# Quarter-array matmuls for filter generation and RG-LRU gates, odd magnitudes on VectorE

## The chip, the cores and the metric

The kernel runs on one core of one Trainium2 chip. The metric is the device time of one execution in microseconds (us), the median of the runs. TensorE multiplies, VectorE (DVE), ScalarE (ACT) and GpSimd (POOL) work on vectors, and SyncE (SP), ACT and POOL issue transfers (DMAs).

## The reference, cut to what matters

One encoder block over 2048 tokens of 1024 channels, all in float32. Half of the mixer is an RG-LRU (a gated linear recurrence, forward and backward), half a Hyena operator (long convolutions with filters that a small network makes). Then comes a mixture of experts, which the change does not touch.

```
# filters: k = [hf, 0, reversed hb], then divided by its own absolute sum
z = sin(ff2 * (z @ fw2 + fb2))                       # 64 features per position
h = (z @ fw3).reshape(seq, 2, 2, 512) * exp(-t * deltas)
k = concat([h[:, 0], 0, h[1:, 1][::-1]])
k = k / (sum(abs(k)) + EPS)
# gates: 8 heads of 64 channels, block-diagonal weights, for each direction
r = sigmoid(einsum("bshi,hij->bshj", xh, wr) + br)
i = sigmoid(einsum("bshi,hij->bshj", xh, wi) + bi)
a = exp(-8 * r * softplus(-lam));  b = sqrt(1 - a*a) * (i * xc)
h = scan(a, b)                                       # forward, and backward with its own weights
```

## The kernel before

Every engine runs its own instruction list in program order, and semaphores are the only links between the lists. The program is a sequence of phases. The change touches two of them, and what it queues on POOL reaches into a third.

**Filters (`norm_and_filters`).** The filter of 4096 positions is worked through in 32 tiles `j` of 128 positions by 2 orders by 512 channels. For each tile TensorE makes the values (`generate`, L229, into one of two PSUM buffers `pk`), DVE multiplies them by the decay table (L374, into one of four buffers `kt`, or `kt0` for tile 0), ACT takes the magnitude (L303, into `ka[j % 2]`), POOL adds it to a running sum (L200), TensorE multiplies the tile by a transform matrix (`transform`, L243), and ACT copies that out (L309) for a store by SP. `zzd` holds the features of both filter halves as a block-diagonal operand padded with zeros, so that one matmul contracts over 128 rows. Every second tile ACT and DVE also split one slice of the normalised input into a high and a low part (`h_hi`, L319; `h_lo`, L355). TensorE issues `generate(j)`, then `transform(j - 2)`; `generate(j)` waits for L374 of tile `j - 2`. After tile 31 TensorE multiplies the sum by ones, DVE adds the skip term to `kt0` (L379, L382), and the last transform follows.

**Projection and RG-LRU (`project_and_lru`).** TensorE projects 20 tiles of 128 channels (L521, 96 matmuls each, in 4 chunks of 512 tokens with one PSUM bank each). Four of them are lru inputs `("x", c)`, four are lru gates `("g", c)`. For every `c`, four gate products of 4 chunks (L534: weights r and i, forward and backward) go through the same 4 banks. Each matmul takes two 64x64 heads as one 128x128 block-diagonal weight `WG`. ACT evacuates them with a sigmoid (L591) into `T` and `I`, DVE multiplies by `xc` (`weigh`, L725), ACT makes decay terms (L634 to L637), DVE scans (L735). The list for one `c` on DVE: `weigh` twice, `lru_input`, forward scan, `low`, `lru_input`, backward scan, `add_directions` (L739), `lru_conv(c + 1)`, `low`, `gate_result` (L744), which signals `y_ready`. ACT begins the sigmoids of `c + 1` when `y_ready` comes. The gates of `c = 0` are interleaved with other work; those of `c` = 1, 2, 3 stand together behind the projection of `("g", c - 1)`. A group of gates also needs the convolved input of its own `c` (`xc_ready`).

**Long convolution (`conv`).** It starts while `c = 3` is being finished. DVE runs the last backward scan after its first block of products (`scan_last`), the sum of directions after its fourth (`add_last`). POOL makes the real part `yr` of each block (L1050, L1054), which TensorE's `inverse` (L957) waits for. This phase's code follows `project_and_lru`'s on every engine.

Of the kernel before, what the change touches and what calls it, by code (L numbers as in the profile page):

```python
# [109 lines left out]
def norm_and_filters(nc, dram, h_hi, h_lo, X, invn, ident):  # L110
# [7 lines left out]
    with ExitStack() as ctx:  # L118
# [5 lines left out]
        zzd = sb("zzd", [P, 2, SEQ])  # L124
# [3 lines left out]
        w3, fa, ones = sb("w3", [P, 2, CH]), sb("fa", [P, P]), sb("ones", [P, P])  # L128
        dec = sb("dec", [P, 4, CH])
# [5 lines left out]
        skip = dec[0:1, 0:2, :]  # L135
# [9 lines left out]
        kgen, k_ready, abs_ready, summed, fa_done, kst_ready = (sem(n, 0) for n in ("kgen", "k_ready", "abs_ready", "summed", "fa_done", "kst_ready"))  # L145
# [10 lines left out]
        def _(sp):  # L156
# [14 lines left out]
            sp.dma_start(fa[:, :], dram["fa_filter"]).then_inc(f_in, 16)  # L171
# [5 lines left out]
            for j in range(N2):  # L177
                if j >= 4:
                    sp.wait_ge(k_ready, j - 3)
                sp.dma_start(dec[:, j % 4, :], dram["decay"][:, j, :]).then_inc(dec_in[j % 4], 16)  # L180
                if j >= 5:
                    store(j - 5)
            sp.wait_ge(k_ready, N2 - 2)
            sp.dma_start(skip, dram["hy_skip"]).then_inc(skip_in, 16)
# [6 lines left out]
        def _(pool):  # L191
# [5 lines left out]
            for j in range(N2):  # L197
                pool.wait_ge(abs_ready, j + 1)
# [4 lines left out]
        def _(pe):  # L203
# [19 lines left out]
            view = zzd.rearrange("p h (q l) -> p l h q", l=N2)  # L223

            def generate(j):
                if j >= 2:
                    pe.wait_ge(k_ready, j - 1)
                for o in range(2):
                    last = pe.matmul(pk[j % 2][:, o, :], view[:, j], w3[:, o, :], start=True, stop=True)  # L229
                last.then_inc(kgen, 1)  # L230

            def transform(i):
# [3 lines left out]
                else:  # L236
                    pe.wait_ge(k0_ready, 1)
# [4 lines left out]
                for o in range(2):  # L242
                    last = pe.matmul(pa[i % 2][:, o, :], fa[:, :], tile(j)[:, o, :], start=True, stop=True)  # L243
# [20 lines left out]
        def _(act):  # L264
# [30 lines left out]
            act.activation(zzd[0:R, 0, :], arg[0:R, :], ACT.Sin).then_inc(mlp_sin, 1)  # L295
            act.activation(zzd[R:P, 1, 1:SEQ][:, ::-1], arg[R:P, 1:SEQ], ACT.Sin).then_inc(mlp_sin, 1)
            turned(FIRST, NT)

            def magnitude(j):
# [3 lines left out]
                act.activation(ka[j % 2], tile(j), ACT.Abs).then_inc(abs_ready, 1)  # L303
# [20 lines left out]
        def _(dve):  # L324
# [32 lines left out]
            dve.memset(zzd[R:P, 0, :], 0.0)  # L357
            dve.memset(zzd[0:R, 1, :], 0.0)
            dve.memset(zzd[R:P, 1, 0:1], 0.0)
# [8 lines left out]
            for j in range(N2):  # L368
                dve.wait_ge(dec_in[j % 4], 16 * (j // 4) + 16)
                dve.wait_ge(kgen, j + 1)  # L370
                if j >= 5:
                    dve.wait_ge(fa_done, j - 4)
                    dve.wait_ge(abs_ready, j - 3)
                dve.tensor_tensor(tile(j), pk[j % 2][:, :, :], dec[:, j % 4, :].unsqueeze(1).broadcast_to([P, 2, CH]), ALU.mult).then_inc(k_ready, 1)  # L374
# [3 lines left out]
            dve.wait_ge(skip_in, 16)  # L378
            dve.scalar_tensor_tensor(out=skip, in0=pk[0][0:1, :, :], scalar=EPS, in1=skip, op0=ALU.add, op1=ALU.mult).then_inc(norm_ready, 1)  # L379
            dve.wait_ge(norm_ready, 1)  # L380
            dve.wait_ge(abs_ready, 1)
            dve.tensor_tensor(kt0[0:1, :, :], kt0[0:1, :, :], skip, ALU.add).then_inc(k0_ready, 1)  # L382
# [13 lines left out]
def project_and_lru(nc, dram, h_hi, h_lo, invn, ident, ps, marks):  # L396


    with ExitStack() as ctx:
# [14 lines left out]
        PT = sb("PT", [P, N_Q + 2, CT])  # L414
# [26 lines left out]
        steps = sem("p_steps")  # L441

# [6 lines left out]
        marks.update(xraw=xraw, WG=WG, fs=fs, mm_done=mm_done, evac=evac, tr_evac=tr_evac, xc_ready=xc_ready, sa_out=sa_out,  # L449
# [58 lines left out]

        @block.tensor
        def _(pe):  # L510
# [16 lines left out]
            def gate(c, g):  # L527
# [43 lines left out]
            for j in range(13, len(TILES)):  # L571
                project(j)
                if TILES[j] in GATED:
                    for g in range(4):
                        gate(GATED[TILES[j]], g)

        @block.scalar
        def _(act):
            col = lambda q, c: PT[:, q, c:c + 1]

# [1450 lines left out]
```

## Time and profile before

| | us |
|---|---|
| median of 3 runs (2303.22 to 2306.31) | 2304.76 |
| the profiled execution | 2303.28 |
| its span in the profile | 2301.5 |
| busy in the span: TensorE / DVE / ACT / POOL | 2068.6 / 1221.4 / 1115.4 / 345.9 |
| filter tiles, first to last `generate` | about 69 to 174 |
| projection and RG-LRU | about 198 to 775 |

The span runs from the first to the last instruction. The granted TensorE clock has a mean of 0.955 of full speed. A matmul of float32 operands stands as two passes in the trace. Starts in the rows are us from the span's start.

### The profile page before, as it was taken

Reading aid. Unit: us, or ns where it says so; the run is one execution under the profiler, and the core shown is the slowest. Engines: PE = TensorE matmul, PEld = TensorE weight load, DVE = VectorE, ACT = ScalarE, POOL = GpSimd, SP = SyncE. Lnnn points to the kernel's source line nnn. Section 1 sums busy time; section 2 is a strip of 40 time slices with the busy share of each in tenths; the row PEclk is TensorE's granted clock in tenths of the full one; section 3 lists DMA queues with packets and bytes.
Section 4 is the critical chain, followed back from the end, with each engine's and each line's share of the span. In section 5 each row is a group of like instructions: output and inputs, shape, how many; then the busy total and the mean of one; then the engine's idle time right before and its main releaser. Section 6 shows DMA issues by size and latency. Waiting matters only on the chain. (4 is left out here: it accounts for less than half of the span.)

```text
span 2301.5 us, 30650 instructions
## 1 busy us (share of the span) xinstructions
PE 2068.6 (90%) x9069; PEld 1500.0 (65%) x9070; DVE 1221.4 (53%) x1111; ACT 1115.4 (48%) x1315; POOL 345.9 (15%) x309
## 2 busy tenths in 40 slices
PE   3996999999999997878999669999999999999990
PEld 1654787786666421226878558888788788888870
DVE  7552322223666654663444475466868655664643
ACT  6762222225555532342333145466867765665643
POOL 0560000000000230220000011212111121221120
PEclk9997999999999999998999769999999999999995
DMA  5461213213111699757542356787999987886858
GB/s 190 157 226 62 64 55 92 73 37 94 39 38 38 244 341 348 273 192 249 178 165 96 128 193 196 249 275 252 374 310 375 374 293 222 297 284 207 291 145 313
DMA packets 239629, 462.08 MB, mean 201 GB/s; under 512 B 24897, under 2 KB 87461, under 8 KB 235174
## 3 DMA queue, kind: packets, MB, share of 16 engines
q1 hardware_dynamic: 201798, 375.17, 45.6%
q0 software_dynamic: 14400, 52.44, 9.5%
q10 hardware_dynamic: 23360, 33.56, 4.5%
q8 instruction: 42, 0.69, 0.1%
q14 instruction: 29, 0.23, 0.0%
HBM read 346.79 MB, written 114.29 MB: 200 GB/s over the span
## 5 line engine op out<-in xcount | busy, mean ns | idle before, releaser
L1762 PE MATMUL p<-wh_hi,x_hi 128*128 128x512 f32 x768 | 309.0, 402 | 1.7 <-DVE x_lo L1876 0.6
L1762 PE MATMUL p<-wh_hi,x_lo 128*128 128x512 f32 x768 | 304.4, 396 | 0.0
L1762 PE MATMUL p<-wh_lo,x_hi 128*128 128x512 f32 x768 | 304.2, 396 | 0.0
L1888 DVE TENSOR_TENSOR wh_lo<-w_raw,wh_hi 128x2048 fp32r<-128x2048 f32 x128 | 284.8, 2286 | 27.6 <-ACT wh_hi L1849 27.6
L521 PE MATMUL ps<-h_hi,wp_hi 128*128 128x512 f32 x640 | 257.7, 403 | 15.3 <-DVE wp_lo L698 15.3
L521 PE MATMUL ps<-h_lo,wp_hi 128*128 128x512 f32 x640 | 254.6, 398 | 0.0
L521 PE MATMUL ps<-h_hi,wp_lo 128*128 128x512 f32 x640 | 254.3, 397 | 0.0
L1849 ACT ACTIVATE wh_hi<-w_raw 128x2048 fp32r<-128x2048 f32 x128 | 234.8, 1924 | 0.4 <-DMA w_raw<-in_exp_w_dram 0.4
L1050 POOL TENSOR_TENSOR arena<-arena 128x512 f32<-128x512 f32 x32 | 56.9, 1778 | 762.4 <-DVE arena L1066 762.4
L1762 PEld LDWEIGHTS p<-wh_hi,x_hi 128*128 128x128 f32 x768 | 144.9, 189 | 35.6 <-issue 1.7
L1762 PEld LDWEIGHTS p<-wh_hi,x_lo 128*128 128x128 f32 x768 | 145.0, 189 | 35.2
L1762 PEld LDWEIGHTS p<-wh_lo,x_hi 128*128 128x128 f32 x768 | 145.0, 189 | 32.8
L1762 PE MATMUL pyy<-wy_hi,a_hi 128*128 x392 | 159.9, 408 | 5.9 <-ACT yb L1833 4.7
L1762 PE MATMUL pyy<-wy_hi,a_lo 128*128 x392 | 155.8, 398 | 0.0
L1762 PE MATMUL pyy<-wy_lo,a_hi 128*128 x392 | 155.6, 397 | 0.0
L521 PEld LDWEIGHTS ps<-h_hi,wp_hi 128*128 128x128 f32 x640 | 121.4, 190 | 46.5 <-DVE wp_lo L698 16.9
L1888 DVE TENSOR_TENSOR wy_lo<-w_raw,wy_hi 128x2048 fp32r<-128x2048 f32 x64 | 144.2, 2286 | 8.8 <-ACT wy_hi L1849 8.8
L1903 DVE TENSOR_TENSOR a<-p,s 128x512 f32<-128x512 f32 x48 | 33.2, 691 | 214.6 <-ACT s L1862 214.6
L521 PEld LDWEIGHTS ps<-h_lo,wp_hi 128*128 128x128 f32 x640 | 121.3, 190 | 29.5 <-issue 1.0
L521 PEld LDWEIGHTS ps<-h_hi,wp_lo 128*128 128x128 f32 x640 | 121.2, 189 | 29.5
L589 ACT ACTIVATE hraw<-ps 128x512 f32<-128x512 f32 x48 | 28.7, 599 | 221.0 <-PE ps L521 221.0
L1849 ACT ACTIVATE wy_hi<-w_raw 128x2048 fp32r<-128x2048 f32 x64 | 120.8, 1923 | 25.0 <-DMA w_raw<-in_exp_w_dram 21.5
(300 smaller groups left out, 3537.0 us busy)
## 6 DMA issues: line engine op xcount, KB each, us to landing
w_raw<-in_exp_w_dram SPq DMA_DIRECT2D x512, 256.0 KB, 5.9
w_raw<-in_exp_w_dram SPq DMA_DIRECT2D x128, 512.0 KB, 10.7
scratch_KA<-work SPq DMA_DIRECT2D x32, 512.0 KB, 3.0
scratch_SI<-arena SPq DMA_DIRECT2D x32, 512.0 KB, 3.4
kin<-scratch_KA SPq DMA_DIRECT2D x21, 512.0 KB, 6.1
arena<-scratch_SA SPq DMA_DIRECT2D x21, 512.0 KB, 5.1
wp_raw<-in_w_in_dram SPq DMA_DIRECT2D x20, 512.0 KB, 3.8
h_raw<-in_x_dram ACTq DMA_DIRECT2D x4, 2048.0 KB, 20.2
```

The lines of the kernel that those rows point to most:

```text
L521: last = pe.matmul(out, w[:, s, k, :], h, start=(k == 0 and i == 0), stop=(k == KC - 1 and i == 2))
L589: ins = act.activation(out[:, 512 * n:512 * (n + 1)], pj[n], func)
L1050: dif = pool.tensor_tensor(yr[:, n % 2, :], by_r[:, n % 2, 0, :], by_i[:, n % 2, 1, :], ALU.subtract)
L1762: mm = pe.matmul(acc[:, :], x[:, k, :], w, start=(k == 0 and i == 0), stop=(k == n - 1 and i == 2))
L1849: act.activation(place, raw[:, j:j + 2, :], ACT.Copy).then_inc(rounded, 1)
L1888: dve.tensor_tensor(lo, raw[:, j:j + 2, :], hi.bitcast(F32), ALU.subtract).then_inc(lowered, 1)
L1903: dve.tensor_tensor(a[:, :], p3[:, :], s1[:, :], ALU.mult).then_inc(a_ready, 1)
```

## The change

The filter values and the gates of `c` = 1, 2, 3 come out of 64x64 quarters of the array, four to a group: two row halves by two column halves. Quarters on the diagonal keep a head (or a filter half) on its partitions; the others put it on the opposite half of the partitions. So half of the results lies swapped.

- Filters: `zz` without padding, four quarter matmuls per tile; order 1 has its partition halves swapped, so the decay table and the transform matrix get a second, swapped copy (512 KB per tile instead of 256 KB). Magnitudes of odd tiles move from ACT to DVE as max(-k, k). The skip term is added in two pieces.
- Gates: for each kind and chunk, four quarters into two banks, forward straight, backward swapped. The backward direction then uses `PT_swapped` and `xc_swapped`, and the result of the backward scan is swapped back. All exchanges are pairs of SBUF to SBUF transfers issued by POOL. `xc_swapped` lies in `xraw`, so its next filling waits for `weighed`.
- On DVE `add_directions(c)` moves behind `lru_conv(c + 1)` and `low`, and waits for `exchanged`.

```
-                    last = pe.matmul(pk[j % 2][:, o, :], view[:, j], w3[:, o, :], start=True, stop=True)
+                    for h in range(2):
+                        rows, out = slice(R * h, R * h + R), slice(R * (h ^ o), R * (h ^ o) + R)
+                        last = pe.matmul(pk[j % 2][out, o, :], view[rows, j], w3[rows, o, :], start=True, stop=True)
...
-            magnitude(1)
...
-                magnitude(j)
+                if j % 2 == 0:
+                    magnitude(j)
...
+                if j % 2:
+                    dve.wait_ge(k_ready, j + 1)
+                    if j >= 3:
+                        dve.wait_ge(summed, j + 1)
+                    dve.scalar_tensor_tensor(out=ka[1], in0=tile(j), scalar=-1.0, in1=tile(j), op0=ALU.mult, op1=ALU.max).then_inc(abs_odd, 1)
...
+            def exchange(out, a, done):
+                for h in range(2):
+                    pool.dma_start(out[halves[h]], a[halves[1 - h]]).then_inc(done, 16)
+
+            pool.wait_ge(lam_ready, 1)
+            exchange(PT_swapped, PT, pt_swapped)
+            for c in range(1, CT):
+                pool.wait_ge(xc_ready, c + 1)
+                exchange(xc_swapped, xc, xc_exchanged)
+                pool.wait_ge(scanned, 2 * c + 2)
+                exchange(I[1], T[1], exchanged)
...
+            def gate_quarters(c):
+                pe.wait_ge(xc_ready, c + 1)
+                pe.wait_ge(wg_in, 16 * 8 * (c + 1))
+                for kind in range(2):
+                    for n in range(NCHUNK):
+                        u = kind * NCHUNK + n
+                        b = 2 * (u % 2)
+                        pe.wait_ge(evac, after(gate_place[c] + u // 2 - 1, b + 1))
+                        for d in range(2):
+                            for h in range(2):
+                                rows, out = halves[h], halves[h ^ d]
+                                last = pe.matmul(pj[b + d][out, :], WG[rows, 2 * d + kind, R * h:R * h + R], xc[rows, n * 512:(n + 1) * 512],
+                                                 start=True, stop=True)
+                            last.then_inc(mm_done, 1)
...
-                dve.wait_ge(evac, after(gate_place[c] + 2 * d + 1))
-                step(dve.tensor_tensor(I[d], I[d], xc, ALU.mult))
+                dve.wait_ge(evac, after(gate_place[c] + (3 if c else 2 * d + 1)))
+                if c and d:
+                    dve.wait_ge(xc_exchanged, 32 * c)
+                    dve.tensor_tensor(I[d], I[d], xc_swapped, ALU.mult).then_inc(weighed, 1)
+                    dve.wait_ge(weighed, c)
...
                 lru_scan(1)
-                add_directions(c)
+                if c == 0:
+                    add_directions(c)
                 lru_conv(c + 1)
                 low(TILES.index(("g", c)) + 1)
+                if c:
+                    add_directions(c)
                 gate_result(c)
```

The built order of instructions shows three places.

On DVE in the filter tiles, before (two tiles; L374 is the decay product, L355 the low part):

```order
L374 TENSOR_TENSOR work<-fk,dec 128x1024 [waits fa_done,abs_ready,kgen,dec_in2]
L355 TENSOR_TENSOR h_lo<-h_raw,h_hi 128x1024 [waits h_high]
L374 TENSOR_TENSOR work<-fk,dec 128x1024 [waits fa_done,abs_ready,kgen,dec_in3]
L374 TENSOR_TENSOR work<-fk,dec 128x1024 [waits fa_done,abs_ready,kgen,dec_in0]
L355 TENSOR_TENSOR h_lo<-h_raw,h_hi 128x1024 [waits h_high]
```

and with the change (L378, L358; L383 is the magnitude of an odd tile):

```order
L378 TENSOR_TENSOR work<-fk,dec 128x1024 [waits fa_done,abs_even,kgen,dec_in2]
L358 TENSOR_TENSOR h_lo<-h_raw,h_hi 128x1024 [waits h_high]
L378 TENSOR_TENSOR work<-fk,dec 128x1024 [waits abs_odd,fa_done,kgen,dec_in3]
L383 SCALAR_TENSOR_TENSOR ka<-work 128x1024 [waits summed,k_ready]
L378 TENSOR_TENSOR work<-fk,dec 128x1024 [waits fa_done,abs_even,kgen,dec_in0]
```

The magnitude stands behind the product of its tile and waits for POOL's sum of the tile two before.

On DVE behind the backward scan of `c = 1`, before (L739 adds the directions, L704 and L706 are the convolution, L744 gates the result):

```order
L735 SCALAR_TENSOR_TENSOR hraw<-tst,hc 128x2048 [waits p_steps]
L739 TENSOR_TENSOR hraw<-hraw 128x2048 [waits scanned]
L704 TENSOR_SCALAR hc<-xraw,PT 128x2048 [waits evac,p_steps]
L706 SCALAR_TENSOR_TENSOR hc<-xraw,PT,hc 128x2048 [waits p_steps] x3
L698 TENSOR_TENSOR wp_lo<-wp_raw,wp_hi 128x1024 [waits w_high]
L744 TENSOR_TENSOR tst<-hraw,spread 128x64x32 [waits evac]
```

and with the change:

```order
L797 SCALAR_TENSOR_TENSOR hraw<-tst,hc 128x2048 [waits p_steps]
L761 TENSOR_SCALAR hc<-xraw,PT 128x2048 [waits evac]
L763 SCALAR_TENSOR_TENSOR hc<-xraw,PT,hc 128x2048 [waits p_steps] x3
L755 TENSOR_TENSOR wp_lo<-wp_raw,wp_hi 128x1024 [waits w_high]
L803 TENSOR_TENSOR hraw<-hraw,hc 128x2048 [waits exchanged,scanned]
L808 TENSOR_TENSOR tst<-hraw,spread 128x64x32 [waits evac,p_steps]
```

The sum moved from before the convolution to behind `low`, with a wait for the exchange.

On POOL, what stands between the sums of the filter phase and the first `yr` of the long convolution, with the change; before, the two memsets were all there was:

```order
L521 MEMSET prow 128x128
L522 MEMSET WG 128x512
L526 DMA PT_swapped<-PT 64x108 [waits lam_ready]
L526 DMA PT_swapped<-PT 64x108
L526 DMA xraw<-hc 64x2048 [waits xc_ready]
L526 DMA xraw<-hc 64x2048
L526 DMA hc<-hraw 64x2048 [waits scanned]
L526 DMA hc<-hraw 64x2048
```

The last four rows come three times, for `c` = 1, 2, 3. So POOL's first `yr` now stands behind a wait for the last backward scan and two transfers.

## Rows read from the trace of the kernel before

**Rows 1.** The page: busy time, share of the span, instructions of each engine.

```profile
PE 2068.6 (90%) x9069; PEld 1500.0 (65%) x9070; DVE 1221.4 (53%) x1111; ACT 1115.4 (48%) x1315; POOL 345.9 (15%) x309
```

**Rows 2.** Windows: length, busy PE, PEld, DVE, ACT, POOL, clock, DMA share, GB/s.

```profile
120.00:150.00 30.00, 30.00 (x72) 17.12 (x71) 14.98 (x13) 21.53 (x23) 20.36 (x10) 1.00 0.72 236
```

**Rows 3.** Timeline of two filter tiles: start, us, engine, line, operation, [idle before, releaser].

```profile
112.42 1.22 DVE L374 TENSOR_TENSOR work<-fk,dec 128x1024 f32<-128x1024 f32 x1 [1.04 <-issue]
...
113.88 1.88 PE L229 MATMUL fk<-w,zzd 128*128 128x512 f32 x4
...
114.81 2.35 POOL L200 TENSOR_TENSOR acc<-acc,ka 128x1024 f32<-128x1024 f32 x1 [1.07 <-ACT ka L303]
...
115.60 1.88 PE L243 MATMUL fp<-work,fa 128*128 128x512 f32 x4
...
115.86 1.22 DVE L374 TENSOR_TENSOR work<-fk,dec 128x1024 f32<-128x1024 f32 x1 [2.21 <-PE fk L229]
...
117.00 1.25 DVE L355 TENSOR_TENSOR h_lo<-h_raw,h_hi 128x1024 fp32r<-128x1024 f32 x1
117.11 1.06 ACT L303 ACTIVATE work<-work 128x1024 f32<-128x1024 f32 x1 [1.46 <-DVE work L374]
```

**Rows 4.** Timeline of the early filter tiles, DVE and POOL side by side.

```profile
81.11 2.37 POOL L200 TENSOR_TENSOR acc<-acc,ka 128x1024 f32<-128x1024 f32 x1
...
82.68 1.88 DVE L355 TENSOR_TENSOR h_lo<-h_raw,h_hi 128x1024 fp32r<-128x1024 f32 x1
...
83.93 2.85 POOL L200 TENSOR_TENSOR acc<-acc,work 128x1024 f32<-128x1024 f32 x1 [0.45 <-ACT work L303]
```

**Rows 5.** Timeline of TensorE in the long convolution, half-array matmuls.

```profile
1012.99 1.89 PE L933 MATMUL ps<-kin,fwd_b 128*64 128x512 f32 x8
1014.81 1.99 PE L957 MATMUL ps<-arena,inv_b 64*128 64x512 f32 x8
1016.72 1.94 PE L944 MATMUL ps<-arena,fwd_b 128*64 128x512 f32 x8
```

**Rows 6.** Timeline of ACT around the gates of `c = 1`.

```profile
610.65 0.60 ACT L589 ACTIVATE spread<-ps 128x512 f32<-128x512 f32 x1 [5.00 <-PE ps L521]
...
615.03 2.42 ACT L591 ACTIVATE hraw<-ps,PT 128x512 f32<-128x512 f32 x4 [2.19 <-DVE tst L744]
...
620.36 0.69 ACT L591 ACTIVATE hraw<-ps,PT 128x512 f32<-128x512 f32 x1 [0.17 <-PE ps L534]
...
627.08 1.28 ACT L634 ACT_TABLE_LOAD   x1
```

**Rows 7.** Timeline from there to the next gates, ACT and DVE.

```profile
633.60 1.91 ACT L637 ACTIVATE hraw<-hraw 128x2048 f32<-128x2048 f32 x1
...
643.16 0.60 ACT L589 ACTIVATE xraw<-ps 128x512 f32<-128x512 f32 x1 [4.05 <-PE ps L521]
...
654.64 4.43 DVE L735 TENSOR_TENSOR_SCAN hraw<-tst,hc 128x2048 f32<-128x2048 f32 x1
...
671.79 3.72 DVE L744 TENSOR_TENSOR tst<-hraw,spread 128x2048 f32<-128x2048 f32 x1 [0.72 <-ACT spread L589]
```

**Rows 8.** A window of 2 us at the start of the long convolution, TensorE alone.

```profile
782.00:784.00 2.00, 1.30 (x4) 0.50 1.11 455
```

**Rows 9.** Timeline there: POOL, DVE, TensorE.

```profile
780.16 4.95 POOL L1054 COPY arena<-arena 1x512 f32<-1x512 f32 x1
780.30 4.41 DVE L735 TENSOR_TENSOR_SCAN hraw<-tst,hc 128x2048 f32<-128x2048 f32 x1
...
786.31 2.94 PE L957 MATMUL ps<-arena,inv_b 64*128 64x512 f32 x8
```

**Rows 10.** A group of POOL's by form: busy us, mean ns of one.

```profile
L1728 POOL DMA_INDIRECT scratch_X<-yb,curspot x50 | 80.3, 1606 | 41.4 <-POOL curspot L1725 39.7 <-PE px L1770 1.7
```

**Rows 11.** Transfers: out<-in, queue, count, KB each, median us to landing.

```profile
scratch_YT<-tst SPq DMA_DIRECT2D x3, 1024.0 KB, 5.1
...
scratch_X<-yb,curspot POOLq DMA_INDIRECT x50, 9.2
```

More of the change, by code:

```diff
@@ L134, in norm_and_filters @@
         ka, acc, kt0 = [kst[:, 3], split(ka1)], split(acc_flat), split(gain)
-        skip = dec[0:1, 0:2, :]
+        skip = [dec[R * o:R * o + 1, 0, o, :] for o in range(2)]
         pair = lambda name: ctx.enter_context(nc.psum_tensor(name, [P, 2, CH], F32))
@@ L183, in _ @@
             sp.wait_ge(k_ready, N2 - 2)
-            sp.dma_start(skip, dram["hy_skip"]).then_inc(skip_in, 16)
+            for o in range(2):
+                sp.dma_start(skip[o], dram["hy_skip"][:, o, :]).then_inc(skip_in, 16)
             for i in range(N2 - 5, N2):
@@ L242, in transform @@
                 for o in range(2):
-                    last = pe.matmul(pa[i % 2][:, o, :], fa[:, :], tile(j)[:, o, :], start=True, stop=True)
+                    last = pe.matmul(pa[i % 2][:, o, :], fa[:, o, :], tile(j)[:, o, :], start=True, stop=True)
                 last.then_inc(fa_done, 1)
@@ L377, in _ @@
             dve.wait_ge(norm_mm, 1)
[L378 to L382, printed above, removed]
+            dve.wait_ge(skip_in, 32)
+            for o in range(2):
+                dve.scalar_tensor_tensor(out=skip[o], in0=pk[0][R * o:R * o + 1, o, :], scalar=EPS, in1=skip[o], op0=ALU.add, op1=ALU.mult).then_inc(norm_ready, 1)
+            dve.wait_ge(norm_ready, 2)
+            dve.wait_ge(abs_even, 1)
+            for o in range(2):
+                first = kt0[R * o:R * o + 1, o, :]
+                dve.tensor_tensor(first, first, skip[o], ALU.add).then_inc(k0_ready, 1)
             for i in range(NT - 2, NT):
@@ L441, in project_and_lru @@
         steps = sem("p_steps")
+        pt_swapped, xc_exchanged, weighed, exchanged = (sem(n, 0) for n in ("pt_swapped", "xc_exchanged", "weighed", "exchanged"))
+        halves = [slice(R * h, R * h + R) for h in range(2)]
         w_v = dram["w_in"].rearrange("o (k p) n -> p (o k) n", p=P)
@@ L573, in _ @@
                 if TILES[j] in GATED:
-                    for g in range(4):
-                        gate(GATED[TILES[j]], g)
+                    gate_quarters(GATED[TILES[j]])
         @block.scalar
@@ L642, in sigmoids, with sigmoid_quarters @@
                     evacuate(gate_place[c] + g, (T, I)[g % 2][g // 2], ACT.Sigmoid, col(q, c))
+            def sigmoid_quarters(c):
+                for kind in range(2):
+                    for n in range(NCHUNK):
+                        u = kind * NCHUNK + n
+                        for d in range(2):
+                            bank = 2 * (u % 2) + d
+                            act.wait_ge(mm_done, after(gate_place[c] + u // 2, bank))
+                            act.activation((T, I)[kind][d][:, 512 * n:512 * (n + 1)], pj[bank], ACT.Sigmoid,
+                                           bias=col_of((Q_BR, Q_BI)[kind][d], c, d)).then_inc(evac, 1)
             high(0)
```

68 lines of the change are left out of this document (40 added, 28 removed).

## The prediction, written before the changed kernel ran

> **What bounds the kernel now.** I read the busy times first: TensorE is busy 90% of the span, no other engine above 53% [rows 1]. So an edit pays where it shortens TensorE's list or a wait of it, and costs where it gives TensorE a new wait.
>
> In the filter tiles the windows show TensorE busy for 30.00 of 30 us at full clock [rows 2]. The timeline gives the pace: two decay products stand 3.43 us apart (112.42, 115.86), which is `generate`, four passes in 1.72 us (113.88 to 115.60), and `transform`, four more [rows 3]. POOL needs 2.35 of the 3.43 us and then waits 1.07 us for a magnitude; DVE waits for TensorE [rows 3]. TensorE is the bound there, and POOL is the next one.
>
> Around the gates of `c = 1` the timeline of ACT shows another pattern. The last chunk of the gate projection is evacuated at 610.65, DVE's `gate_result` ends 0.02 us before the sigmoids start at 615.03, and the 16 sigmoids end at 627.08 [rows 6]. Four of them from a filled PSUM take 2.42 us, so 0.58 us follows 0.58 us; the rest waits 0.17 us each for a matmul and comes every 0.86 us, the time of two passes [rows 6, 3]. So TensorE sets the gates' pace and ACT could go half again as fast. The next gates come 60.5 us later (615.03 to 671.79 + 3.72 = 675.51), and DVE had 0.72 us of slack before `gate_result` [rows 7].
>
> **The change part by part.**
>
> *Width of the quarters.* No quarter stands in the trace, but halves do. Eight half passes take 1.82 us when they split the columns (1012.99 to 1014.81) and 1.91 us when they split the rows (to 1016.72) [rows 5], against 1.72 us for four full ones [rows 3]. So two go side by side in either direction, with 0.1 to 0.2 us for the changeover. Eight quarter passes then cost 0.86 us if four go side by side, 1.72 if two do, 3.44 if none does. I take 0.86 us plus 0.15.
>
> The Trainium skill's page "TensorEngine Tiling (Array Packing)", section "Restrictions and Gotchas", speaks against that: different row tiles may not use one PSUM bank at the same time, and here both row halves write one bank, on different partitions. The rows of half matmuls don't decide it, since those that split the rows write two banks.
>
> *Filter tiles.* TensorE's work falls from 3.43 to 1.72 + 0.86 + about 0.3 for two changeovers = 2.9 us. Is it still the bound? POOL and DVE hinder each other. While POOL's sum of 81.11 runs (to 83.48), DVE's low part, with two operands in SBUF, takes 1.88 us instead of 1.25: it ends 1.08 us after POOL does. The next sum takes 2.85 instead of 2.35, and ends 2.22 us after the low part [rows 4, 3]. So what starts second stands nearly still. The decay product reads one operand from PSUM and keeps its 1.22 us. Today per pair of tiles 2 x 2.35 + 1.25 = 6.0 of 6.87 us need this resource, and the low part fits in POOL's gap. The moved magnitude has two SBUF operands too (the tile twice) and 1024 elements, 1.22 us. The chain of a pair becomes: magnitude behind a sum 1.07, signal 0.06, sum 2.35, low part behind it 1.10, sum behind that 2.22: 6.8 us, or 3.40 per tile. TensorE's saving of 0.5 us per tile turns into a wait of DVE for POOL. Over the 29 tiles of steady state: 29 x (3.40 - 3.43) = -0.9 us. At the start the first `generate` is 0.86 us shorter, -0.9. Against that stand 0.3 us for the split skip term and 0.5 us for 1 MB more of decay data beside the loading of the input. Sum of the stage: -1.0 us. Bounds: no hindrance below (rival 1), other order above (rival 2).
>
> The Trainium skill's page "SBUF — State Buffer", section "SBUF: two separate sides", gives the same mechanism as an exclusive lock, held for a whole instruction, between GpSimd and a VectorE instruction with two SBUF inputs. By full durations the pair would be 2 x 2.35 + 1.22 + 1.25 = 7.2 us, 3.6 per tile, and the stage 5 us slower; the rows show 0.14 us less at each handover, and the rows decide.
>
> The transfers per tile grow from 768 KB to 1 MB. At 0.72 share for 236 GB/s [rows 2], 1.05 MB takes 3.2 us of full share, at the 455 GB/s seen for 1.11 [rows 8] 2.6. Both are under 3.40, so they hide; they would not hide under a pace of 2.9.
>
> *Gates of c = 1, 2, 3.* `gate_result`'s end is 0. Two groups of quarters (four banks) are done before. ACT takes the first four chunks in 2.42 us. The banks come free two at a time, TensorE refills them in about 1.0 us, plus 0.17 until ACT sees it [rows 6]; ACT meanwhile has two chunks, 1.15 us. That makes about 2.5 us per four chunks: 2.5 x 3 + 2.42 = 10.0 us instead of 12.05. TensorE may go on when the first chunk of the last four has left its bank, at about 8.4, instead of 10.7 (it is one pass behind the sigmoids today): -2.25 us. DVE now multiplies both directions after all sigmoids: 10.0 + 2 x 2.3 = 14.6, while ACT needs 8.4 us from the sigmoids to the end of its square root (627.08 to 633.60 + 1.91) [rows 6, 7], so 18.4. So this is hidden by ACT; without that cover it would cost 2.3. `evacuate` of the next lru input waits for `weighed` at 14.6, before ACT gets there anyway. The second half of the cycle follows TensorE's third chunk (643.16) [rows 7] and moves with it.
>
> The backward scan ends at 659.07 [rows 7]. The convolution and `low` behind it keep DVE busy for about 9.7 us, and the sum has another 0.7 us of slack. In that time the exchange of 1 MB must land. The nearest rows: 1024 KB on SP's queue in 5.1 us, POOL's scatter in 9.2 [rows 11], and 1.6 us to issue each of two [rows 10]. 1.6 + 5.1 = 6.7 is hidden; 1.6 + 9.2 = 10.8 is late by 0.4. I take it as hidden. The exchange of `xc` has some 20 us. Sum of three groups: 3 x -2.25 = -6.75, and 0.25 comes back because ACT's last evacuation gains only 2.05: -6.5 us. Bounds: 0 (two quarters at a time) and 3 x (12.05 - 16 x 0.58) = -8.
>
> *Start of the long convolution.* This is the price. POOL's first `yr` used to be ready before 785.11, with `inverse` at 786.31 on TensorE [rows 9]. Now POOL's list first waits for the last backward scan, which ends at 784.71, and issues two transfers, 2 x 1.6 us [rows 10]. Then come the difference (half of 2.35, 1.2) and the copy (0.4): 789.5. Everything of this phase stands behind that `inverse` on TensorE: +3.2 us. Lower bound 0 (an issue that costs nothing ends at 786.3), upper bound 6, with the 1 MB (2.3 us at 455 GB/s) among the loads that TensorE waits for [rows 8].
>
> *Sum.* -1.0 - 6.5 + 3.2 = -4.3 us. The profiled execution took 2303.28, so 2299.0; it lay 1.5 us under the median of 2304.76, which makes a median of **2300.5 us**. For this case alone 2295 to 2308. The measurement tells about 0.2%, 4.6 us, from no change.
>
> **The rivals.**
>
> 1. *The magnitude doesn't hinder POOL* (it reads one tile, so perhaps one stream). For it: no instruction of its form runs beside POOL in the trace. Against: every two-operand one does stall. Then TensorE's 2.9 or the transfers' 2.6 to 3.2 bound a tile; with 3.0 the stage gains 29 x 0.43 = 12.5 instead of 0.9, in all -16: 2289. Chance 0.17.
> 2. *The sum wins the resource before the low part* (slower). The low part is issued when ACT starts the next magnitude, 1.06 us before the next sum is ready [rows 3], so it should be first; if POOL gets in first, the order is sum 2.35, low part 1.10, product 1.22, magnitude 1.28, sum 2.4: 8.3 us a pair, 4.17 a tile, +0.74 x 29 = 21. In all 2322. It decides at the end of each odd tile's sum: who starts there. Chance 0.14.
> 3. *Fewer than four quarters at a time.* Two: a tile takes 1.72 + 1.72 + 0.15 = 3.6, +5, the gates gain nothing, +3.2: 2313. Only the middle two of four, as the bank rule would have it: 2.6 us a group, 4.5 a tile, +30; gates 8 x 2.6 instead of 13.7, +21: 2359. Chance 0.13 together, mostly the first.
> 4. *TensorE's clock falls in the gates.* With quarters it fills its banks in 2 us and then idles 4. In the window from 782 it starts again after a wait (busy 1.30 of 2 us), and the granted clock is 0.50, 1.2 GHz [rows 8]. At that level three groups take 2.1 instead of 1.25 us, 2.5 per `c`, and the gates' gain is gone: 2307. Chance 0.10.
> 5. *The exchange lands late* by 1 us or more in two cycles, 2303 to 2310. Chance 0.05.
>
> **How the numbers follow.** The forecast's own case has 0.41. Half of it lies below -0.2%, half within. Faster: 0.20 + 0.16 (rival 1) + 0.01 = 0.37. Within: 0.20 + 0.09 (rivals 4, 5) = 0.29. Slower: 0.34, from rivals 2 and 3, from part of 4 and 5, and from a filter stage between 3.4 and 4.2 per tile. The range from 2284 to 2318 holds the own case, rival 1, rivals 4 and 5, two quarters at a time and a mixed order in rival 2.
>
> **What would show it.** Right: quarter groups of about 1.0 us; decay products about 3.4 us apart with TensorE idle some 0.5 us a tile; magnitudes of odd tiles of 1.9 to 2.3 us beside POOL's sums; sigmoids over in 10 us; POOL's first `yr` behind two transfers, and TensorE waiting for it before `inverse`. Wrong: odd magnitudes of 1.2 us beside a running sum (rival 1), low parts that wait behind two sums (rival 2), or a group of quarters of 1.7 us and more (rival 3).

## The result, and the profile after

The changed kernel takes 2310.62 us (median of 13 runs, 2307.49 to 2314.24), the kernel before, measured beside it, 2304.76 (13 runs): ratio 1.0025, 95% interval 1.0017 to 1.0033. It is slower by 0.25%, a little more than can be told from no change. The forecast was 2300.5. Its wide range, 2284 to 2318, holds the result; the 2295 to 2308 given for the forecast's own case does not, and the direction was wrong. The page of the profiled execution, span and busy times, beside [rows 1]:

```profile
span 2309.2 us, 31121 instructions
PE 2046.6 (89%) x9293; PEld 1456.3 (63%) x9294; DVE 1247.6 (54%) x1127; ACT 1096.2 (47%) x1299; POOL 376.8 (16%) x323
```

The span grew by 7.7 us (2301.5 before), although TensorE works 22 us less: its work turned into waits. This is one execution of each kernel; the medians differ by 5.9 us. The timeline of a pair of filter tiles (start, us, engine, line, operation, [idle before, releaser]):

```profile
103.75 1.21 DVE L378 TENSOR_TENSOR work<-fk,dec 128x1024 f32<-128x1024 f32 x1
...
106.16 1.23 DVE L383 SCALAR_TENSOR_TENSOR ka<-work 128x1024 f32<-128x1024 f32 x1 [1.19 <-POOL acc L201]
106.20 3.40 POOL L201 TENSOR_TENSOR acc<-acc,work 128x1024 f32<-128x1024 f32 x1
...
106.93 1.16 PE L232 MATMUL fk<-w,zz 64*64 64x512 f32 x8
...
108.44 2.25 DVE L358 TENSOR_TENSOR h_lo<-h_raw,h_hi 128x1024 fp32r<-128x1024 f32 x1
108.57 1.98 PE L246 MATMUL fp<-work,fa 128*128 128x512 f32 x4 [0.48 <-DVE work L378]
...
109.74 3.17 POOL L201 TENSOR_TENSOR acc<-acc,ka 128x1024 f32<-128x1024 f32 x1
```

and a window there, answering to [rows 2] (length, busy PE, PEld, which is TensorE's weight load, DVE, ACT, POOL, clock, DMA share, GB/s):

```profile
120.00:150.00 30.00, 26.66 (x107) 8.83 (x106) 25.19 (x19) 15.68 (x17) 28.85 (x9) 1.00 0.90 304
```

Eight quarter passes take 1.16 us. Two decay products that are two tiles apart start 6.85 us apart (103.75 to 110.60), 3.42 per tile as before, but POOL is now busy 28.85 of 30 us and TensorE 26.66. The magnitude waits for the sum that reads its buffer; the next sum starts 0.04 us behind the magnitude and takes 3.40 instead of 2.35; the low part takes 2.25 instead of 1.25, and the sum behind it 3.17. The end of that stage, first as a timeline:

```profile
178.24 2.34 POOL L201 TENSOR_TENSOR acc<-acc,ka 128x1024 f32<-128x1024 f32 x1
180.72 3.75 PE L258 MATMUL fk<-acc,ones 128*128 128x512 f32 x4 [5.20 <-POOL acc L201]
184.27 3.41 PE L262 MATMUL fk<-ones,acc 128*128 128x2 f32 x16
...
190.60 3.78 PE L246 MATMUL fp<-gain,fa 128*128 128x512 f32 x4 [2.92 <-DVE gain L394]
...
210.41 0.80 PE L548 MATMUL ps<-h_hi,wp_hi 128*128 128x512 f32 x1 [16.03 <-DVE wp_lo L755]
```

The window (length, busy PE, PEld, DVE, ACT, POOL, clock, DMA share, GB/s):

```profile
180.00:185.00 5.00, 4.28 (x9) 2.25 (x9) 0.00 (x0) 0.00 (x0) 0.57 (x1) 0.50 0.00 0
```

TensorE comes out of a wait of 5.20 us at a granted clock of 0.50, 1.2 GHz. In the kernel before the wait was 1.54 us, and the same two groups took 1.95 and 1.84 us:

```profile
179.11 1.95 PE L255 MATMUL fk<-acc,ones 128*128 128x512 f32 x4 [1.54 <-POOL acc L200]
180.90 1.84 PE L259 MATMUL fk<-ones,acc 128*128 128x2 f32 x16
...
185.29 3.78 PE L243 MATMUL fp<-gain,fa 128*128 128x512 f32 x4 [2.55 <-DVE gain L382]
```

In the changed kernel they start 1.61 us later than before (180.72 for 179.11), the last transform 5.31 us later, the first projection 6.06 (210.41 for 204.35). ACT in the gates of `c = 1`:

```profile
618.95 0.69 ACT L693 ACTIVATE hraw<-ps,PT 128x512 f32<-128x512 f32 x1 [1.97 <-DVE tst L808]
...
622.29 0.69 ACT L693 ACTIVATE hraw<-ps,PT 128x512 f32<-128x512 f32 x1 [0.91 <-PE ps L574]
...
624.00 0.69 ACT L693 ACTIVATE hraw<-ps,PT 128x512 f32<-128x512 f32 x1 [0.44 <-PE ps L574]
...
629.89 0.68 ACT L693 ACTIVATE hc<-ps,PT_swapped 128x512 f32<-128x512 f32 x1
```

A window in it:

```profile
622.00:624.00 2.00, 2.00 (x16) 0.62 (x12) 0.00 (x0) 1.27 (x3) 0.00 (x0) 0.50 1.15 348
```

Against [rows 6]: the 16 sigmoids take 11.64 us instead of 12.05, since TensorE fills two banks every 1.71 us at 1.2 GHz and ACT waits for it. Last, the start of the long convolution, beside [rows 9], and a window of it:

```profile
784.46 1.01 POOL L526 DMA_DIRECT2D hc<-hraw  x2 [53.61 <-DVE hraw L797]
785.49 1.28 POOL L1117 TENSOR_TENSOR arena<-arena 128x512 f32<-128x512 f32 x1
...
787.93 1.99 PE L1024 MATMUL ps<-arena,inv_b 64*128 64x512 f32 x8 [2.71 <-POOL arena L1121]
...
796.84 3.45 PE L1000 MATMUL ps<-xraw,fwd_b 128*64 128x512 f32 x8 [5.05 <-DMA xraw<-scratch_KA]
```

The window:

```profile
788.00:794.00 6.00, 3.79 (x16) 1.17 (x16) 2.33 (x2) 2.21 (x3) 1.02 (x1) 1.00 1.03 239
```

The two transfers cost POOL 1.01 us to issue, and TensorE then waits 2.71 us for POOL. But the fourth filter product (the first starts at 769.75, the second at 775.81) waits another 5.05 us for its data, behind the exchange: it starts at 796.84 and before at 791.19, where no wait of TensorE is listed. In the window the DMA engines are fully busy and move 239 GB/s; before, the same window had 402:

```profile
791.19 1.94 PE L933 MATMUL ps<-xraw,fwd_b 128*64 128x512 f32 x8
...
788.00:794.00 6.00, 5.92 (x26) 1.70 (x24) 2.98 (x3) 2.20 (x3) 1.37 (x2) 0.98 1.06 402
```

### The profile page after: what moved, and what is told of

It reads as the page before. It is cut to its first block and busy times, and to the rows that moved or that the text cites. A ratio compares the mean times of both kernels' runs of the same rounds, so it can differ in the third digit from the quotient of the medians.

```text
span 2309.2 us, 31121 instructions
## 1 busy us (share of the span) xinstructions
PE 2046.6 (89%) x9293; PEld 1456.3 (63%) x9294; DVE 1247.6 (54%) x1127; ACT 1096.2 (47%) x1299; POOL 376.8 (16%) x323
## 5 line engine op out<-in xcount | busy, mean ns | idle before, releaser
L1792 POOL COPY curspot<-spot 128x1 int32 x50 | 43.9, 877 | 528.1 <-ACT yb L1900 528.1
```

The source lines that it names most:

```text
L1792: pool.tensor_copy(cur_spot[:, :], spot[:, ds(B, 1)]).then_inc(spot_ready, 1)
```

## The experiments

The ratios below are to the kernel before, measured beside each experiment; each interval is 0.1 to 0.2% wide to either side. The code shows the lines that matter of each edit, and `...` marks what is left out.

**One half of the change at a time.** e1 keeps the filters and takes the gates of before, e2 the reverse.

```diff
-                    gate_quarters(GATED[TILES[j]])
+                    for g in range(4):
+                        gate(GATED[TILES[j]], g)
...
```

> The filter part of the change alone, gates and directions as before. Theory: the filter stage is where most of the loss arises. Its pace stays near 3.42 us a tile because DVE's new magnitudes and POOL's sums hinder each other, its tail costs 1.6 us on POOL and 3.4 us on TensorE at the lower clock, so that the first projection matmul starts at about 210.4 instead of 204.4 (+6), and the whole is 4 to 6 us slower than before. The load of the last exchange is absent, so the third filter product of the long convolution waits no longer than before. Rival (the loss comes from the gates and their exchanges): within 1 us of before.

Measured: 1.0009 (0.9999 to 1.0019). The first projection starts 5.8 us late, as the theory said; the whole is not the expected 4 to 6 us slower but 2, which can't be told from no change. By the second filter product the lag is 2.4 us. The wait for `xraw` at the fourth is 1.71 us.

> The gate part alone, filters as before. Theory: the three groups of gates gain about 3.5 us, then TensorE waits some 5 us for a load at its fourth filter product of the long convolution, behind the last exchange of 1 MB, and that with the lower clock behind it costs 6.5: in all 2 to 4 us slower than before. Rival (the wait is bad luck in the phase of the loads, not of the exchange, or arises from the shifted filter stage): no such wait, and 2 to 4 us faster than before.

Measured: 1.0015 (1.0003 to 1.0027). At the convolution's second filter product this kernel is 5.1 us ahead of the one before (770.32 for 775.40), and a wait of 4.71 us for `xraw` takes that back. The two halves add up to the whole (0.09 and 0.15% against 0.25%), and neither pays.

**All magnitudes back on ACT.**

```diff
-                if j % 2 == 0:
-                    magnitude(j)
+                magnitude(j)
```

> The whole change, but all magnitudes stay on ACT. Theory (DVE and POOL hinder each other): POOL's sums go back to about 2.4 us, the pace falls to 2.9 to 3.1 us a tile, the stage gains 10 to 13 us on the change, and TensorE's clock may stay up in its tail, another 3: 10 to 16 us less than the change, 5 to 10 under before. Rival (the transfers, 1 MB a tile, set the pace): 3.2 to 3.4 us a tile, 1 to 6 us less than the change. Rival (TensorE with its changes of array mode sets it): as the first, but TensorE without idle time.

Measured: 0.9960 (0.9946 to 0.9974). Timeline of two tiles:

```profile
110.00 1.23 DVE L378 TENSOR_TENSOR work<-fk,dec 128x1024 f32<-128x1024 f32 x1 [1.78 <-PE fk L232]
...
113.00 1.23 DVE L378 TENSOR_TENSOR work<-fk,dec 128x1024 f32<-128x1024 f32 x1 [0.64 <-issue]
```

A window of 30 us there:

```profile
90.00:120.00 30.00, 30.00 (x121) 10.23 (x120) 17.87 (x16) 24.40 (x26) 28.57 (x11) 1.00 1.00 351
```

3.00 us a tile instead of 3.42. TensorE and the DMA engines are full, and POOL, 28.57 of 30 us, nearly so; which of them would hold a still shorter tile is open. The moved magnitude, not the quarters, held the stage.

**The last gates on the full array**, so that no exchange stands ahead of the convolution.

```diff
-            for c in range(1, CT):
+            for c in range(1, CT - 1):
                 pool.wait_ge(xc_ready, c + 1)
...
-            sp.wait_ge(marks["weighed"], CT - 1)
+            sp.wait_ge(marks["xc_ready"], CT)
```

> The whole change, but the last group of gates (c = 3) is computed on the full array as before, so that its exchanges fall away. Theory (the last exchange of 1 MB delays the loads of the long convolution): TensorE's wait of 5 us at its fourth filter product is gone, -6.5 us, the gates of c = 3 lose their gain, +1.1: 5 to 6 us less than the change, about equal to before. Rival (the exchange is hidden, the loads are late for another reason): +1 us against the change.

Measured: 1.0004 (0.9995 to 1.0014), 0.21% (4.8 us) under the change, although the gates of `c = 3` give up their gain. The wait of 5.05 us is 0.99.

**Both corrections**, the edits of e3 and e4 together.

> This is the changed kernel with both corrections of the third and fourth run: all magnitudes on ACT (the third gave 2294.96 us, 15.7 less than the change) and the gates of the last c on the full array as before, so that no exchange stands ahead of the long convolution (the fourth gave 2304.24, 6.4 less). Theory (the two losses lie in different stages and are independent): the savings add up, 2310.6 - 15.7 - 6.4 = 2288.5 us, and in the trace the sums of the filter tiles come every 3.0 us and no wait of TensorE for xraw above 2 us stands at the start of the long convolution. Rival (the third run has already taken part of the second's saving, since its wait for xraw was 4.1 instead of 5.1 us): 2290 to 2292. Either way it beats the kernel before by 0.5% or more.

Measured: 2289.1 us, 0.9937 (0.9921 to 0.9954). The savings add up: 0.65% of e3 and 0.21% of e4 under the change's 1.0025 make 0.9939. The wait for `xraw` is 0.16 us.

**What the exchange costs by itself.** The kernel before, with the exchange added: e6 with 512 KB a transfer, e7 with 32 KB.

```diff
+            pool.wait_ge(scanned, 2 * CT)
+            for h in range(2):
+                pool.dma_start(I[1][halves[h]], T[1][halves[1 - h]]).then_inc(exchanged, 16)
...
+                if c + 1 == CT:
+                    dve.wait_ge(exchanged, 32)
```

In e7 the transfer is this:

```diff
+                pool.dma_start(I[1][halves[h]][:, 0:128], T[1][halves[1 - h]][:, 0:128]).then_inc(exchanged, 16)
```

> The kernel before, with one thing added: after the last backward scan POOL issues two transfers of 512 KB from SBUF to SBUF, the load of the last exchange, into a buffer that nobody reads; DVE's last sum of directions waits for them. Nothing is left out of the computation. Theory (the transfer itself displaces the loads of the long convolution): a wait of TensorE for xraw of 4 to 5 us appears among its first four filter products, and the time rises by 4 to 6 us, to about 2310. Rival (the wait in the changed kernel has another reason, such as the earlier arrival of the gates or the later first load, which here stays as before): no wait above 2 us and a time within 2 us of before, apart from at most 1 us for POOL's issue.

> As the run before it, but the two added transfers carry 32 KB each instead of 512 KB, so that POOL issues as many and DVE waits at the same place. Nothing is left out of the computation. Theory (the bytes are what costs): no wait of TensorE for xraw above 2 us and a time within 1.5 us of before. Rival (the issue by POOL, or its place in the queue, is what costs): the same wait of 4 to 5 us and the same 4 to 6 us as with the full size.

Measured: e6 1.0030 (1.0020 to 1.0040), e7 1.0005 (0.9994 to 1.0015). The intervals do not touch: the bytes cost, not the issue. Timeline of e6, then its window:

```profile
797.52 3.68 PE L940 MATMUL ps<-xraw,fwd_b 128*64 128x512 f32 x8 [5.57 <-DMA xraw<-scratch_KA]
```

Its window there:

```profile
788.00:794.00 6.00, 3.96 (x16) 1.13 (x15) 2.17 (x2) 2.21 (x3) 0.82 (x1) 0.96 1.03 230
```

**Why it costs that much.** Each edit is against e6. A megabyte read from HBM instead (e9), the exchange by SyncE's queue (e13), in pieces of 2 KB (e14), and a megabyte from HBM over 128 partitions in such pieces (e15):

```diff
-                pool.dma_start(I[1][halves[h]], T[1][halves[1 - h]]).then_inc(exchanged, 16)
# e9
+                pool.dma_start(I[1][halves[h]], x_rows[halves[1 - h], 0:SEQ]).then_inc(exchanged, 16)
# e13
+                sp.dma_start(I[1][halves[h]], T[1][halves[1 - h]]).then_inc(exchanged, 16)
# e14
+                out = I[1][halves[h]].rearrange("p (a n) -> p a n", n=CH)
+                pool.dma_start(out, T[1][halves[1 - h]].rearrange("p (a n) -> p a n", n=CH)[:, ::-1]).then_inc(exchanged, 16)
# e15
+                out = I[1][:, 2 * CH * h:2 * CH * (h + 1)].rearrange("p (a n) -> p a n", n=CH)
+                pool.dma_start(out, x_rows[:, 2 * h:2 * h + 2, 0]).then_inc(exchanged, 16)
```

> As the run with the full exchange added to the kernel before, but the two added transfers of 512 KB read from HBM (1 MB of the input x) instead of from SBUF, by the same queue, at the same place and into the same idle buffer. Nothing is left out of the computation. There the DMA engines moved only 220 to 240 GB/s at full share while the exchange ran, against 390 to 420 without it. Theory (a transfer from SBUF to SBUF takes twice the engine time of a load of the same size): the rate stays near 400 GB/s, the wait of TensorE for xraw shrinks from 5.6 us to 2 to 3, and the time is 2 to 3 us over before, 2305 to 2306. Rival (any megabyte at this place costs the same, since it goes ahead of the filter's loads): a wait of 5 to 6 us and a time as with the exchange, 1.0030 of before.

> The kernel before with the full exchange of 1 MB added at the same moment (after the last backward scan), but issued by SyncE's queue, behind the loads that it issues near 779 us and ahead of the store near 790, instead of by POOL's. Nothing is left out of the computation. With POOL's queue both an exchange and a load from HBM halved the rate of the DMA engines (220 to 240 and 208 to 253 GB/s at full share, against 390 to 420), and the profile's page of the kernel before has the same 240 GB/s for all of POOL's transfers (52.44 MB in 9.5% of the span). Theory (POOL's queue is what makes a byte cost about 1.7 times as much): the rate stays at 330 GB/s or more, the wait for xraw is 2 to 4 us, and the time 1 to 3 us over before. Rival (the form of the transfer, long rows of 64 partitions at a time, is what costs): the rate falls to 210 to 260 GB/s again, and the wait and the time are as with POOL's queue, 5 us and 1.003 of before.

> The kernel before with the full exchange of 1 MB added by POOL's queue, as in the sixth run, but each row of 8 KB is cut into four pieces of 2 KB (written in reversed order, into the same idle buffer), which is the length of a row in the filter's loads. Nothing is left out of the computation. Rows of 8 KB halved the rate from POOL's and from SyncE's queue, and from SBUF as from HBM. Theory (the length of the pieces makes a byte cost more): the rate between 788 and 794 us stays at 330 GB/s or more instead of 230, and the wait for xraw falls from 5.6 to 2 to 3.5 us. Rival (64 partitions at a time, or any transfer that lands in SBUF here beside the loads): 220 to 260 GB/s again and a wait of 5 to 6 us.

> The kernel before with 1 MB from HBM added by POOL's queue at the same place, as in the ninth run, but each of its two transfers covers all 128 partitions with two pieces of 2 KB, the form of the filter's own loads. Nothing is left out of the computation. Theory (the form of the rows costs): 380 GB/s or more between 788 and 794 us, a wait for xraw of 2 to 3 us where the ninth run had 3.5, and a time within 3 us of before. Rival (POOL's queue or any added load at this place halves the rate): 210 to 260 GB/s and the wait of 3.5 us or more again.

The window from 788 to 794 us of e9:

```profile
788.00:794.00 6.00, 5.11 (x16) 1.31 (x14) 1.01 (x1) 2.21 (x3) 0.67 (x1) 0.75 1.03 234
```

The same of e13:

```profile
788.00:794.00 6.00, 3.71 (x19) 0.93 (x17) 3.05 (x3) 2.20 (x3) 1.29 (x2) 1.00 1.06 249
```

The same of e14:

```profile
788.00:794.00 6.00, 5.50 (x16) 1.64 (x16) 0.63 (x1) 2.07 (x3) 1.04 (x1) 0.72 1.05 251
```

The same of e15:

```profile
788.00:794.00 6.00, 3.66 (x10) 1.26 (x8) 2.10 (x2) 0.00 (x0) 3.76 (x4) 0.50 1.01 397
```

Three of my theories fell: the rate is as low from HBM, from the other queue, and in short pieces. Only the transfer over all partitions keeps 397 GB/s. POOL's own DMA queue says the same, whatever the edges of the window. Its last two transfers in the changed kernel, from 765 to 830 us (packets, MB, share of the time of 16 engines):

```profile
q0 software_dynamic: 160, 1.05, 7.0%
```

That is 4.6 us of all 16 engines. The same row for e6, e9 and e14 from 775 to 805 us has 15.4, 14.7 and 14.4%, which is 4.6, 4.4 and 4.3 us; for e15 it has 9.0%, 2.7 us. What the three slow ones share with the exchange is 64 partitions at a time; that the width alone does it is not shown, since e15 differs from e9 in its pieces too, and from e14 in its source.

The times don't follow the rate as closely: 1.0019 (e9), 1.0021 (e13), 1.0027 (e14) and 1.0019 (e15), with intervals that overlap each other and that of e6. The waits for `xraw` at the fourth filter product are 3.50 us in e9, 2.29 in e13 and 2.39 in e14, against 5.57 in e6 and 0.78 in e7; in these three they came out as the theories had it or between theory and rival, and only the rates were the rivals'. e15, at the full rate, is 0.19% slower (1.0008 to 1.0031), and there TensorE waits 2.34 us for POOL and not for `xraw`. Its trace does not tell why, since it is 2.5 us late at the first filter product already, ahead of the added load. So that the bytes cost time is shown (e6 against e7); that the low rate is what makes them cost it is not.

**TensorE kept busy in its wait**, on the changed kernel (e8).

```diff
+            for _ in range(10):
+                pe.matmul(pk[1][:, 1, 0:2 * P], ones[:, :], fa[:, :, :], start=True, stop=True)
             pe.wait_ge(summed, N2 + 2)
```

> The changed kernel, with ten idle matmuls of 256 columns (ones times the transform table, into columns of PSUM that nobody reads) on TensorE where it waits 5.2 us for the last sum of magnitudes. By the first projection rows they take some 0.43 us each, 4.3 in all. Nothing is left out of the computation. Theory (the tail of the filter stage is late because TensorE comes out of that wait at 1.2 GHz): the four matmuls with ones take 1.95 us instead of 3.75 and the sixteen small ones 1.84 instead of 3.41, as in the kernel before; the last transform starts 3 to 3.5 us earlier and the whole takes 2307.3. Rival (the clock falls all the same, because the engine was slow or idle elsewhere): the rows stay at 3.75 and 3.41 and the time does not move.

Timeline of TensorE there:

```profile
180.29 1.98 PE L260 MATMUL fk<-acc,ones 128*128 128x512 f32 x4 [0.81 <-POOL acc L201]
182.11 1.84 PE L264 MATMUL fk<-ones,acc 128*128 128x2 f32 x16
186.87 3.78 PE L246 MATMUL fp<-gain,fa 128*128 128x512 f32 x4 [2.92 <-DVE gain L396]
```

Its window, to be laid beside that of the changed kernel:

```profile
180.00:185.00 5.00, 3.66 (x20) 2.62 (x20) 0.98 (x2) 0.00 (x0) 0.24 (x1) 1.00 0.00 0
```

The clock stays at 2.4 GHz, and the last transform comes 3.73 us earlier. Of these 0.34 are there already when the last sum ends; 3.4 us of the tail is the clock. The time does not follow: 2309.51 us, 1.0026 (1.0016 to 1.0036), for 2307.3 expected. The last sigmoids still start 2.6 us earlier, and then the waits at the convolution's start are 5.12 and 6.92 us; its fourth filter product starts at 797.01, in the changed kernel at 796.84. There the transfers set the time, and what is gained ahead of them is lost.

**The pace of the filter tiles.** e10 makes the odd magnitude with one operand, e11 moves the low parts behind the loop.

```diff
-                    dve.scalar_tensor_tensor(out=ka[1], in0=tile(j), scalar=-1.0, in1=tile(j), op0=ALU.mult, op1=ALU.max).then_inc(abs_odd, 1)
+                    dve.tensor_scalar(ka[1].bitcast(mybir.dt.int32), tile(j).bitcast(mybir.dt.int32), 0x7fffffff, None, ALU.bitwise_and).then_inc(abs_odd, 1)
```

> The changed kernel, with VectorE's magnitude of the odd tiles made with one operand in SBUF (the sign bit masked off) instead of two (the larger of x and -x). The result is the same bit for bit. Theory (the pace of 3.42 us a tile comes from two-operand instructions of VectorE and POOL that hold each other up): the even sums fall from 3.40 to 2.35 us, the pace to 3.0 us, the bound by TensorE and the transfers, and the time by 29 x 0.42 = 12 us, to about 2298. Rival (the pace comes from the order itself: the magnitude waits for the sum that reads its buffer, and the next sum for it): the magnitude still stands between two sums and POOL idles beside it, 6.2 to 6.8 us a pair, and the time falls by 9 us at most, or not at all.

Timeline of VectorE and POOL in e10:

```profile
105.51 0.70 DVE L383 TENSOR_SCALAR ka<-work 128x1024 int32<-128x1024 int32 x1 [1.20 <-POOL acc L201]
105.55 2.87 POOL L201 TENSOR_TENSOR acc<-acc,work 128x1024 f32<-128x1024 f32 x1
...
108.56 3.17 POOL L201 TENSOR_TENSOR acc<-acc,ka 128x1024 f32<-128x1024 f32 x1
```

Measured: 2301.38 us, 0.9982 (0.9973 to 0.9992), 6.32 us a pair. The theory half fell: POOL's sum is not free of a one-operand instruction either, it is longer by 0.5 us of the 0.66 in which that still runs. The magnitude is shorter, and that is the gain: 0.43%, 9.9 us under the change, where the theory had 12 and the rival at most 9.

```diff
-                if j >= 4 and j % 2 == 0:
-                    low_part(j // 2 - 2)
...
-            for i in range(NT - 2, NT):
+            for i in range(NT):
                 low_part(i)
```

> The changed kernel, with VectorE's sixteen low parts moved behind the tile loop, so that only the magnitudes stand against POOL's sums. Nothing is left out of the computation. Theory: without the low part the odd sums take 2.35 instead of 3.17 us and a pair 3.40 + 2.35 + 0.2 = 6.0 us, 3.0 a tile, as without the magnitudes; the last sum starts near 166 instead of 178 us, and fourteen low parts of 1.2 us each behind the last transform eat that up, so the whole stays within 6 us of the changed kernel. Rival (the magnitude alone is what slows the stage): the pace stays above 3.3 us and the whole gets slower by 12 us or more.

Timeline of POOL's sums in e11:

```profile
104.26 3.41 POOL L201 TENSOR_TENSOR acc<-acc,work 128x1024 f32<-128x1024 f32 x1
...
107.81 2.37 POOL L201 TENSOR_TENSOR acc<-acc,ka 128x1024 f32<-128x1024 f32 x1
```

Measured: 1.0033 (1.0019 to 1.0047). As the theory said: odd sums of 2.37, 3.03 us a tile, and the sixteen low parts behind the loop (18.25 us from 179.51) eat it up.

**The best version**: e5 with five of e8's idle matmuls.

> The fifth run's kernel (all magnitudes on ACT, gates of the last c on the full array; 2289.1 us) with five idle matmuls of 256 columns on TensorE while it waits 3.2 us for the last sum. Theory: the matmuls with ones take 1.95 instead of 3.25 us, and what follows up to the last transform about 2.5 us less in all, and since no transfer is late at the start of the long convolution the whole falls by as much, to 2286.6. Rival (the projection's length varies by 2 us between kernels, and a gain of this size ahead of it isn't seen in the whole, as in the eighth run): the local rows shorten, the time stays at 2289 within 1.5 us.

Measured: 2286.52 us, 0.9921 (0.9908 to 0.9933), for 2286.6 forecast. That the value fits so well is partly luck, since the kernel before measured 2305.03 beside this one and 2302.94 beside e5. The last transform starts 2.2 us earlier than in e5. The interval overlaps e5's, so the last step is likely and not proven.

## Why the prediction failed

*Width of the quarters*: right. Four go side by side, 1.16 us for eight, though both row halves write one PSUM bank; so the bank rule of rival 3 does not hold TensorE up here. TensorE's tile is 3.00 us where I had 2.9 (e3, where no wait of TensorE is listed).

*Filter tiles, pace*: right, 3.42 for 3.40, and rival 2 did not come. The magnitudes do not stretch to 1.9 to 2.3 us as I expected; they wait for their buffer, start first, and POOL's sum stretches. That it is these VectorE instructions beside POOL is shown by e3, e10 and e11. The Trainium skill's page "SBUF — State Buffer", section "SBUF: two separate sides", says that of a GpSimd instruction and a VectorE instruction with two SBUF inputs the later one is blocked for the whole of the first; the sums of 3.40 us, 1.05 longer than alone behind a magnitude of 1.23, agree with it within 0.2 us.

*"Sum of the stage: -1.0 us"*: the first step that failed; it was +6.1. Three things were missing. The chain of sums is the bound from the first tile on, while before the first four sums followed each other every 2.5 us: the last starts 1.6 us later. TensorE now waits 5.20 us for it (1.54 before) and comes back at 1.2 GHz, worth 3.4 us (e8). The split skip term takes 0.4 for the 0.3 that I had, and the change to the next stage 0.75 more, for a reason that no run isolates. I had costed TensorE's new idle time at nothing because POOL covers it; it had a price where the cover ends.

*Gates, "-6.5 us"*: mis-sized, -3.5. The gains are 0.8, 1.6 and 1.1 us for `c` = 1, 2, 3 (59.75 and 58.92 from sigmoids to sigmoids against 60.5). The missing part is rival 4, the clock at 1.2 GHz at the head of the group, where TensorE fills two banks in 1.71 us, no faster than full passes at 2.4 GHz. ACT waits 1.8, 1.0 and 0.9 us for TensorE there in the three groups; without these waits each would take the 10 us that I had. In the windows of 2 us with these waits the granted clock is 0.50 to 0.62. No run holds the clock up in a group, so this cause is read from the rows. In the second half of `c = 1`'s group the clock is back and ACT sets the pace again (mostly 0.57 to 0.59 us from chunk to chunk). The exchanges of the first two groups were hidden, as forecast: DVE's sum of `c = 1` starts at 671.66, straight behind `low`.

*Start of the long convolution, "+3.2 us"*: the second step that failed, +6.7 by the lags below. The issue, priced by POOL's indirect transfers [rows 10], cost 1.0 us instead of 3.2, and the delay of `inverse` was 1.6 (787.93 for 786.31). The load of the exchange, which I had only in the upper bound with 2.3 us and did not take, cost about 5 (e6 less e7: 0.25%, 5.8 us; e4: 4.8, with the gain of a group of gates given up). It runs at half the rate that I had read in [rows 8], though e15 leaves open how much of the cost is the rate. The Trainium skill's page "SBUF — State Buffer", section "Door 1: The DMA port swizzle", states that partitions 0 to 63 reach only 8 of the 16 ports into SBUF, and 64 to 127 the other 8. By that 1 MB in two halves, if they do not run side by side, would cost 4.6 us of full rate, as an estimate, instead of 2.3. The runs agree: 4.3 to 4.6 us of all engines for the transfers of 64 partitions at a time and 2.7 for the two over all 128.

*The sum*, as the changed kernel's lag behind the kernel before: first projection +6.1; sigmoids of `c` = 1, 2, 3 +3.9, +3.2, +1.5; second filter product +0.4 (775.81 for 775.40), fourth +5.6, POOL's sum behind it +7.2, since that product runs at 1.2 GHz and takes 3.45 instead of 1.94 us; end +7.7. Against the forecast the filter stage was 7.1 us worse, the gates 3.0 and the start of the convolution 3.5.

By these the sum would be -4.3 + 7.1 + 3.0 + 3.5 = +9.3. The projection stage took back 2.1 of it (from +6.1 to +3.9), which I had not forecast: without it the result would have been further off. It goes with TensorE's granted clock. Windows of 190 us, the kernel before and then the changed one:

```profile
410.00:600.00 190.00, 184.58 (x793) 140.65 (x792) 69.94 (x34) 72.23 (x102) 0.00 (x0) 0.98 0.23 65
410.00:600.00 190.00, 184.62 (x807) 140.57 (x806) 66.01 (x33) 72.28 (x101) 0.00 (x0) 1.00 0.23 65
```

In the kernel before the granted clock is 0.83 from 440 to 450 us and 0.66 from 525 to 530, 3.4 us lost; in the changed kernel it is 1.00 in both. From the first projection to the sigmoids of `c = 1` the five traces without such a fall (the change, e1, e2, e4, e11) take 407.3 to 408.6 us. Of the eight with the same loss, seven (the kernel before, e3, e6, e8, e10, e13, e14) take 410.2 to 410.7, and e12 407.9. What makes the clock fall there is open, and so is whether the change brings the 2.1 us each time.

## What to carry to other kernels

Work moved off the bound engine is free only while its cover lasts: look at what that engine does on coming back from the wait, its clock first. A transfer's price is what it does to the transfers around it, and where the DMA engines are full a megabyte must be priced, by the engine time of a transfer of its own form. Test halves of a change alone: here one edit inside it (the magnitudes) was worth 15 us in the other direction.

## What I had not expected of the hardware

Beside a transfer between halves of the partitions the DMA engines are at a share of 1.03 while they move 230 GB/s (e6); a loaded engine share says nothing of the rate. A one-operand VectorE instruction of 0.70 us also makes POOL's sum longer (2.87 instead of 2.37 us, e10). Four quarter passes run at once although both row halves write one PSUM bank (1.16 us for eight).
